# Expert results added in memory by the scatter, in two sums, in a fused mixing and MoE layer

## The reference

```
h = rmsnorm(x, norm_ffn_pre) * (1 + sc2) + sh2
y = moe_ffn(h)            # 64 experts, each token goes to 8 of them
x = x + gt2 * rmsnorm(y, norm_ffn_post)

moe_ffn: idx, gate = grouped top-8 of sigmoid(h @ w_router)
         routed[token] = sum over its 8 experts e of
                         gate * ((silu(h @ we_gate[e]) * (h @ we_up[e])) @ we_down[e])
         shared        = (silu(h @ ws_gate) * (h @ ws_up)) @ ws_down
         y = routed + shared
```

## Time and profile before

| | |
|---|---|
| runs | 1507.34, 1509.97, 1515.13 us; median 1509.97 |
| the profiled execution | 1509.81 us, of which its span is 1508.0 us |
| TensorE busy, share of the span | 1352.0 us, 90% |
| VectorE | 1045.0 us, 69% |
| ScalarE | 613.3 us, 41% |
| GpSimd | 344.7 us, 23% |
| device memory read, written | 334.40 MB, 44.04 MB |
| mean granted TensorE clock | 0.938 of full speed |

### The profile page before, as it was taken

One profiled execution on the slowest core, in us unless ns is written; L12 is line 12 of the kernel. 1 busy time (PEld: TensorE's weight loads), 2 busy tenths in 40 slices (PEclk: granted clock), 3 DMA queues, 4 the chain that ended last, 5 costly groups with the idle time before them and its releaser, 6 DMA issues. The chain is left out here.

```text
span 1508.0 us, 18807 instructions
## 1 busy us (share of the span) xinstructions
PE 1352.0 (90%) x5795; PEld 926.9 (61%) x5795; DVE 1045.0 (69%) x1646; ACT 613.3 (41%) x928; POOL 344.7 (23%) x350
## 2 busy tenths in 40 slices
PE   6799999965589799869699999999999999999947
PEld 3577676723589544344476777777777777776713
DVE  4539999959833252325688887887888888888617
ACT  3322222142123211211465565665665665655502
POOL 0344324133000000000223232232232333232200
PEclk9799999876699899979799999999999999999969
DMA  8343534110000440094289999989999988999358
GB/s 305 144 148 131 202 133 146 49 70 0 1 1 1 168 167 14 28 355 196 78 330 346 364 352 347 359 349 347 365 384 368 356 343 348 361 351 338 143 212 352
DMA packets 85841, 341.34 MB, mean 226 GB/s; under 512 B 16983, under 2 KB 20241, under 8 KB 58661
## 3 DMA queue, kind: packets, MB, share of 16 engines
q1 hardware_dynamic: 65976, 307.07, 53.2%
q0 software_dynamic: 19584, 33.60, 6.2%
q10 hardware_dynamic: 236, 0.09, 0.0%
HBM read 334.40 MB, written 44.04 MB: 251 GB/s over the span
## 5 line engine op out<-in xcount | busy, mean ns | idle before, releaser
L2144 DVE TENSOR_TENSOR gate_up_low<-gate_up,gate_up_high 128x1024 fp32r<-128x1024 f32 x204 | 245.3, 1223 | 47.2 <-ACT gate_up_high L2035 41.9
L2116 PE MATMUL py<-down_ring,hT 128*128 128x512 f32 x544 | 250.0, 602 | 0.9 <-ACT hT L2054 0.9
L2077 PE MATMUL p_gate_up<-gate_up_high,x_hi 128*128 128x512 f32 x544 | 242.7, 446 | 5.3 <-DVE x_lo L2153 5.3
L2077 PE MATMUL p_gate_up<-gate_up_low,x_hi 128*128 128x512 f32 x544 | 216.6, 398 | 0.0
L2077 PE MATMUL p_gate_up<-gate_up_high,x_lo 128*128 128x512 f32 x544 | 216.6, 398 | 0.0
L2035 ACT ACTIVATE gate_up_high<-gate_up 128x1024 fp32r<-128x1024 f32 x204 | 204.1, 1052 | 1.0 <-issue 0.8
L2116 PEld LDWEIGHTS py<-down_ring,hT 128*128 128x128 f32 x544 | 97.9, 190 | 98.8 <-issue 98.7
L2006 POOL TENSOR_TENSOR carrier<-offsets 1x1 f32<-1x1 f32 x136 | 28.7, 211 | 535.9 <-DVE tokens L2162 487.3
L269 POOL TENSOR_TENSOR ring_lo<-ring,w_hi 128x2048 fp32r<-128x2048 f32 x19 | 91.6, 4823 | 179.0 <-ACT w_hi L310 179.0
L2077 PEld LDWEIGHTS p_gate_up<-gate_up_high,x_hi 128*128 128x128 f32 x544 | 104.0, 191 | 45.6 <-issue 21.2
L429 PE MATMUL pz<-h_hi,w_hi 128*128 128x512 f32 x304 | 123.4, 406 | 7.7 <-DVE h_lo L497 7.7
(11 more groups left out here) (363 smaller groups left out, 2034.8 us busy)
## 6 DMA issues: line engine op xcount, KB each, us to landing
down_ring<-in_we_down SPq DMA_DIRECT2D x68, 1024.0 KB, 8.7
gate_up<-in_we_gate SPq DMA_DIRECT2D x51, 1024.0 KB
gate_up<-in_we_up SPq DMA_DIRECT2D x51, 1024.0 KB
ring<-in_w_ada SPq DMA_DIRECT2D x12, 2048.0 KB, 8.1
ring<-in_w_in SPq DMA_DIRECT2D x9, 2048.0 KB, 10.4
x_again<-in_we_gate SPq DMA_DIRECT2D x17, 1024.0 KB
x_again<-in_we_up SPq DMA_DIRECT2D x17, 1024.0 KB
rows<-expert_rows SPq DMA_DIRECT2D x6, 2048.0 KB, 18.4
```

The costliest lines, as they stand in the source:

```text
L2077: mm = pe.matmul(pgu[u % 2][:, :], x[:, u % 2, k, :], weights, start=(k == 0 and n == 0), stop=(k == KD - 1 and n == 2))
L2116: mm = pe.matmul(py[half][:, :], hT[:, u % 2, k, :], weights[:, k, half * N:half * N + N], start=(k == 0), stop=(k == 1))
L2144: V.tensor_tensor(moe.low[u % RING][:, :, piece(i), :], moe.gate_up[u % RING][:, :, piece(i), :], exact(w_hi[:, u % 2, :, piece(i), :]), A ...
```

## The change

- The row numbers go: the table has two values for each pair of token and expert (gate and token), and the scan, the subtraction and the four additions that built the third value are gone.
- `expert_rows` (4096 rows) is replaced by two arrays `expert_sums0` and `expert_sums1` of 512 rows. The scatter's target is the token's own row, in the first array for even blocks and the second for odd ones, and the DMA adds to what is there.
- In `route` SP first writes zeros to the second array (8 DMAs of 256 KB) ahead of the experts' first weights, and behind these weights writes the shared expert's result to the first array (4 DMAs of 512 KB, each when ScalarE has copied its tile). It waits for the zeros at the end of the stage. The first scatter waits for the shared rows.
- The residual's tile is its own and no longer a slot of the ring; in `route` it holds the shared expert's result. SP loads the residual after the weights of block 63, ahead of those of the extra blocks.
- `combine` loads two rows a token (8 DMAs of 512 KB, 4 MB in all). TensorE has no part in it. VectorE adds the two, and finishes tile t - 1 behind the sums and gates of tile t.

```diff
 # route
             sp.dma_start(wsd[:, :, :], ...)
+            sp.wait_ge(s_zero, 1)
+            for t in range(NT):
+                for half in range(2):
+                    sp.dma_start(moe.sums[1][t * P:(t + 1) * P, half * N:half * N + N], nothing).then_inc(s_clear, 16)
             for b in range(moe.RING):
                 moe.load_gate_up(sp, b, b)
                 moe.load_down(sp, b, b)
+            for t in range(NT):
+                sp.wait_ge(s_dnA, 2 * t + 2)
+                sp.dma_start(moe.sums[0][t * P:(t + 1) * P, :], shared[:, t, :]).then_inc(moe.s_base, 16)
+            sp.wait_ge(s_clear, 16 * 2 * NT)
...
+            pool.memset(nothing, 0.0).then_inc(s_zero, 1)
...
-            link(V.tensor_tensor_scan(rank[...], resets[...], sel[...], 0.0, ALU.mult, ALU.add))
-            link(V.tensor_tensor(rank[:, :, :], rank[:, :, :], sel[:, :, :], ALU.subtract))
-            for t in range(NT):
-                link.sign(V.tensor_scalar(values[:, t * NE:(t + 1) * NE, 2], rank[:, t, :], tokf[:, 2, t:t + 1], None, ALU.add))
 # experts, SP
+            sp.wait_ge(moe.s_base, 16 * NT)
+            sp.dma_start(moe.x1[:, :, :], keep.x1_dram.rearrange("(t p) d -> p t d", p=P)).then_inc(moe.s_x1, 16)
             count = sp.value_load(moe.n_blocks[0:1, 0:1], min_val=NE, max_val=MAXB)
...
-            sp.wait_ge(s_y, count)
-            sp.dma_start(moe.x1[:, :, :], keep.x1_dram.rearrange("(t p) d -> p t d", p=P)).then_inc(s_x1, 16)
-            sp.wait_ge(s_x1, 16)
 # experts, scatter
+                if isinstance(b, int) and b == 0:
+                    pool.wait_ge(moe.s_base, 16 * NT)
-                pool.indirect_dma_start(moe.rows, bass.IndirectOffsetOnAxis(row_ids[:, u % 4, 0:1], 0), y[:, u % 2, :], None,
-                                        bounds_check=last_row, oob_is_err=False).then_inc(s_out[u % 2], 16)
+                pool.indirect_dma_start(moe.sums[u % 2], bass.IndirectOffsetOnAxis(targets[:, u % 4, 0:1], 0), y[:, u % 2, :], None,
+                                        bounds_check=last_token, oob_is_err=False, compute_op=ALU.add).then_inc(s_out[u % 2], 16)
 # combine
+            for t in range(NT):
+                for i in range(2):
+                    sp.dma_start(halves[:, i, t, :], moe.sums[i][t * P:(t + 1) * P, :]).then_inc(s_in[t], 16)
...
+                V.tensor_tensor(y[:, t, cols(half)], halves[:, 0, t, cols(half)], halves[:, 1, t, cols(half)], ALU.add).then_inc(s_y, 1)
...
+            for t in range(NT):
+                dve.wait_ge(s_in[t], 32)
+                for half in range(2):
+                    add(t, half)
+                for half in range(2):
+                    gated(t, half)
+                if t:
+                    finish(t - 1)
+            finish(NT - 1)
```

More of the change, by code:

```diff
@@ L1535 @@
 MAXB = NE + S * TOPK // P - 1
-NO_TOKEN, NO_ROW = 8 * S, 16 * S * TOPK
+NO_TOKEN = 8 * S
 BIG = 1e30
@@ L1569, in route @@
         wsd, wr, g8 = old(2, D), old(KD, NE), old(NT, NG, 8)
-        scores, biased, sel, gated, left, rank, resets = (old(NT, NE) for _ in range(7))
+        scores, biased, sel, gated, left = (old(NT, NE) for _ in range(5))
         gs, top4, top8 = (m.sb(n, [P, NT, 8]) for n in ("gs", "top4", "top8"))
@@ L1573, in route @@
         gmask = m.sb("gmask", [P, NT, NG])
+        shared, nothing = moe.x1, old(N)
         total, over = m.sb("total", [P, NT]), m.sb("over", [P, NT])
-        toki, tokf, pi, pf = m.sb("toki", [P, NT], I32), m.sb("tokf", [P, 3, NT]), m.sb("pi", [P, 1], I32), m.sb("pf", [P, 1])
+        toki, tokf, pi, pf = m.sb("toki", [P, NT], I32), m.sb("tokf", [P, 2, NT]), m.sb("pi", [P, 1], I32), m.sb("pf", [P, 1])
         iota_i = m.sb("iota_i", [P, S], I32)
-        values = m.sb("table_values", [P, NT * NE, 3])
+        values = m.sb("table_values", [P, NT * NE, 2])
         colf, before = m.sb("colf4", [P, P]), m.sb("before", [P, P])
@@ L1645, in _ @@
                 for half in range(2):
-                    act.activation(moe.shared[:, t, half * N:half * N + N], bank[6 + half][:, :], ACT.Copy).then_inc(s_dnA, 1)
+                    act.activation(shared[:, t, half * N:half * N + N], bank[6 + half][:, :], ACT.Copy).then_inc(s_dnA, 1)
         @block.tensor
@@ L1849, in plan_experts @@
     moe.n_blocks = m.sb("n_blocks", [1, 1], I32)
-    moe.offsets = m.sb("offsets", [P, 2])
+    moe.offsets = m.sb("no_token", [P, 1])
     moe.s_gate_up = [m.sem(f"expert_gate_up{i}_in") for i in range(moe.RING)]
     moe.s_down = [m.sem(f"expert_down{i}_in") for i in range(moe.RING)]
-    moe.rows = nc.dram_tensor("expert_rows", (S * TOPK, D), F32, kind="Internal").ap()
+    moe.sums = [nc.dram_tensor(f"expert_sums{i}", (S, D), F32, kind="Internal").ap() for i in range(2)]
     halves = [w["we_gate"][0].rearrange("e (p k) n -> e p k n", k=KD), w["we_up"][0].rearrange("e (p k) n -> e p k n", k=KD)]
@@ L1879, in experts @@
         hot = m.sb("hot", [P, 2, NT, P], BF16)
-        column = m.sb("column", [P, 2, NT, 9], BF16)
-        number = m.sb("number", [P, 4, 3])
+        column = m.sb("column", [P, 2, NT, 6], BF16)
+        number = m.sb("number", [P, 4, 2])
         tokens = m.sb("tokens", [P, 4, 1], U32)
-        row_ids = m.sb("row_ids", [P, 4, 1], U32)
+        targets = m.sb("targets", [P, 4, 1], U32)
         x_hi, x_lo = m.sb("x_hi", [P, 2, KD, P], F32R), m.sb("x_lo", [P, 2, KD, P], F32R)
@@ L2104, in numbers @@
                 for t in range(NT):
-                    mm = pe.matmul(pid[:, 0:9], hot[:, u % 2, t, :], column[:, u % 2, t, :], start=(t == 0), stop=(t == NT - 1))
+                    mm = pe.matmul(pid[:, 0:6], hot[:, u % 2, t, :], column[:, u % 2, t, :], start=(t == 0), stop=(t == NT - 1))
                 mm.then_inc(s_id, 1)
@@ L2199, in combine @@
         whole, rstd = m.sb("whole6", [P, NT]), m.sb("rstd6", [P, NT])
[L2200 to L2205, removed]
+        s_in = [m.sem(f"p6_sums{t}_in") for t in range(NT)]
         s_y, s_gt = m.sem("p6_y"), m.sem("p6_y_gated")
@@ L2230, in _ @@
             sp.wait_ge(s_st, 16 * 2 * NT)
[L2232 to L2235, removed]
-                    pe.matmul(bank[2 * t + half][:, :], keep.ident[:, :], moe.shared[:, t, cols(half)], start=True, stop=False)
-                    pe.wait_ge(s_pe_in[t + half if t == LAST else t], 16)
-                    for j in range(H):
-                        mm = pe.matmul(bank[2 * t + half][:, :], keep.ident[:, :], rows[:, t, j, cols(half)],
-                                       start=False, stop=(j == H - 1))
-                    mm.then_inc(s_sum, 1)
         @block.gpsimd
@@ L2296, in finish @@
                                            in1=x1[:, t, cols(half)], op0=ALU.mult, op1=ALU.add).then_inc(s_o, 1)
-            for t in range(LAST):
-                dve.wait_ge(s_dve_in[t], 16)
-                tree(t, slice(0, D))
+            for t in range(NT):
+                dve.wait_ge(s_in[t], 32)
                 for half in range(2):
@@ L2304, in _ @@
                     gated(t, half)
-                finish(t)
-            for half in range(2):
-                dve.wait_ge(s_dve_in[LAST + half], 16)
-                tree(LAST, cols(half))
-                add(LAST, half)
-            for half in range(2):
-                gated(LAST, half)
-            finish(LAST)
+                if t:
+                    finish(t - 1)
+            finish(NT - 1)
 class Names:
```

67 lines of the change are left out of this document (18 added, 49 removed).

## The result

| | before | after |
|---|---|---|
| median of four runs | 1508.74 us | 1546.63 us |
| range of the runs | 1507.34 to 1515.13 | 1537.84 to 1550.87 |
| profiled execution, its span | 1509.81, 1508.0 us | 1546.62, 1544.8 us |

The ratio is 1.0229 (95% interval 1.0181 to 1.0277): slower, and the interval leaves open whether by 2%. The forecast was 1478.3 us, within 1472 to 1496, with 0.85 on faster. It was wrong by 68 us, and in sign.

What follows compares the result with a forecast made beforehand. The prediction took loads to bound the last stage and TensorE the middle stretch, with DMA at 0.92. Last stage -29.1, gap -3.0, expert stage 0 and `route` +0.4 gave -31.7 us: 1478.3 us, range 1472 to 1496.

Steps and rivals of the forecast that it cites:

- The expert stage: 0: Expert stage: no time gained or lost, since the adding scatters' extra DMA work fits under TensorE's time.
- m = 2.2: Expert stage: m is an adding scatter's cost in plain ones; above 2.2 its extra passes 0.83 us a block.
- the ring of four slots: Expert stage, DMA-bound rival: the ring holds about 10 us in reserve, taken once off the loss over 62 blocks.
- The DMA engines become the bound of the expert stage: Rival, blocks 4 to 65: slower, whole gain lost at m = 3.2, 1545 us at m = 4; chance 0.14.
- Last stage, 52.5 to 23.4 us: Last stage: fewer loads, no TensorE products, VectorE the bound after first loads; 29.1 us gained, bounds 25 to 30.
- m = 2: Expert stage: an adding scatter costs two plain ones, one more read of the same 4 KB; bounds 1 and 4.
- Mean DMA share 0.98 with TensorE at 600 of 600: Sign for "right", stretch 770 to 1370: DMA share near 0.98, TensorE still busy 600 of 600 us.
- The sign named for "wrong": Expert stage: idle before a DMA in ScalarE's weight split, or before a scatter in copies to `y`, or a DMA-entered chain.
- The gap, -3.0 us: Between last scatter and last barrier: 3.0 us less as the residual's load moves forward; bounds 0 and -3.8.
- `route`, +0.4 us: End of `route`: SP must issue the last shared write before the barrier, 0.4 us more; bounds 0 and +1.5.
- Latency of the slot, residual and clears hidden: Expert stage and `route`: slot waits, the residual's 5.9 us weight delay and the clears' about 6 us cost 0.
- The sum: Whole kernel: -29.1 - 3.0 + 0 + 0.4 = -31.7 us, giving 1478.3 us.

Runs made afterwards that it cites:

- spread_after: The changed kernel with a block's place 2m put in partition m and place 2m + 1 in partition 64 + m; 1479.59 us.
- plain_scatter: The changed kernel with plain scatters that write over the sum and add nothing, so the sums are left out; 1475.87 us.
- add_even: The changed kernel, places not dealt out, with only even blocks' scatters adding and odd blocks' writing plainly; 1508.61 us.
- two_writes: The kernel before with each scatter issued a second time, plainly, into an array nobody reads; a slot of `y` waits for both; 1592.04 us.
- two_writes_spread: The kernel before with each scatter issued twice, the second into an unread array, and place 2m in partition m, 2m + 1 in 64 + m; 1513.3 us.

## Why the prediction was wrong

**The step that failed** is the free time of DMA. The prediction says "DMA leaves 0.08 x 10.3 = 0.83 us a block free", and in "The expert stage: 0" that "DMA becomes the bound when that passes 0.83 us, at m = 2.2". The share of DMA is a mean over 16 engines, and I spent the free time of all 16 on work that falls mostly to eight. With the same rows, bytes and additions the time is 1547 us with the rows at the front and 1480 us with them spread, so the fullest engines are the bound and not the mean.

Two sizes were wrong, and both come from the mean. The added price on a busy engine is 7.5 x 0.166 = 1.25 us a block, where the mean has 0.62. And the reserve of these engines was not 0.83 us. Two doses measure it: over some 62 blocks the full dose asks for 77 us and took 67 (1547 against spread_after's 1480), the half dose asks for 39 and took 29 (1509). Both leave about 10 us in all, the once-only reserve that the prediction gives to the ring of four slots, or at most 0.16 us a block. Measured from plain_scatter's 1476 instead it is 6 us. I had put add_even in a range that supposed more.

An estimate of the fullest engine's work goes with this. The 3.15 MB of weights a block at 417 GB/s, the rate of the weight loads in 670 to 690 of the kernel before,

```profile
670.00:690.00 20.00, 19.47 (x48) 8.66 (x47) 8.93 (x71) 2.13 (x5) 0.00 (x0) 1.00 1.01 417
```

take 7.54 us on every engine. To it come, on the fullest, 7.5 gathered rows and 7.5 scattered ones of 183 or 349 ns (5.0 each when spread):

| kernel | fullest engine, worked out | a block, measured | time |
|---|---|---|---|
| before | 7.54 + 15 x 0.183 = 10.3 us | 10.3 (TensorE) | 1509 |
| after | 7.54 + 7.5 x 0.183 + 7.5 x 0.349 = 11.5 | 11.4 | 1547 |
| add_even | the mean of these two = 10.9 | 10.7 | 1509 |
| spread_after | 7.54 + 5.0 x 0.183 + 5.0 x 0.349 = 10.2 | 10.3 (TensorE) | 1480 |
| two_writes | 7.54 + 22.5 x 0.183 = 11.7 | 11.5 (52 scatters in 600 us) | 1592 |
| two_writes_spread | 7.54 + 15 x 0.183 = 10.3 | 10.3 (TensorE) | 1513 |

The estimate ranks the kernels, and its sizes are rough. In the mix the weights take more engine time than alone: in the kernel before 0.92 x 10.3 = 9.5 us of mean share less 1.4 us of rows are 8.1 us a block. With 8.1 for 7.54 each row of the table would rise by 0.6 us, above TensorE's 10.3 even where TensorE never waits. Records of a trace can be missing, too, so counts of blocks are good to one or two in a hundred.

**The rival was right in time and wrong in its reason.** "The DMA engines become the bound of the expert stage" stood at 0.14, with 1545 us at m = 4; the measured time is 1547 at m = 1.9. Its sum of 67 us takes an addition of three plain rows less 0.83 us of free time, 1.24 us a block on the mean; the fullest engines were asked for 1.25 us with no more than 0.16 to spare. That the two agree is luck. That DMA would bind, in the stage and at the cost of the whole gain, was the rival's and was right.

**Point by point.**
- *Last stage, 52.5 to 23.4 us:* right, 23.1 us; the additions take 1.28 or 1.29 us a pair (the row of 0.69 us that I read for them gave 1.38), loads 5.1 us to the first addition.
- *m = 2:* right, 1.9. The rule of the Trainium skill ("Collectives: The Full Stack", section "The bandwidth ceiling: the fold count and why AG ≠ RS ≠ AR"), that a reducing DMA runs at half a copy's rate, agrees with this price; no run here separates the read from the addition.
- *Mean DMA share 0.98 with TensorE at 600 of 600:* not in the changed kernel, but exactly what spread_after shows. The sign named in the prediction ("DMA share near 0.98") did not appear: the share fell to 0.90. The sign named for "wrong" did: idle time of the weight split before a DMA.
- *The gap, -3.0 us:* too large. In the changed kernel the gap is 1521.73 - 1509.18 = 12.6 us from the last scatter's issue, 1.2 less than before; and the issue itself comes late. The rows of the end of its expert stage:

```profile
1501.91 1.56 POOL L2021 DMA_INDIRECT expert_sums<-y,targets  x1 [0.46 <-issue]
1508.54 0.18 POOL L2003 TENSOR_TENSOR carrier<-no_token 1x1 f32<-1x1 f32 x1 [5.07 <-DMA expert_sums<-y,targets]
1509.18 1.56 POOL L2021 DMA_INDIRECT expert_sums<-y,targets  x1 [0.46 <-issue]
```
```profile
1505.21 0.69 DVE L2182 COPY y<-py 128x512 f32<-128x512 f32 x1 [4.19 <-PE py L2115]
```

  The rows were ready at 1505.9, and POOL stood until 1508.5 in the wait for the scatter before. I had looked at the gathers behind that wait and not at the next scatter. An issue takes 1.56 us instead of 0.99 too. plain_scatter, with the same order and no addition, has 1449.55 - 1439.76 = 9.8 us, which is the forecast's bound for "nothing added", 13.7 - 3.8 = 9.9. So the addition costs the last scatter 2.8 us here (3.2 in spread_after), where I had given it 0.5. POOL's row and the chain's first in plain_scatter:

```profile
1439.76 0.99 POOL L2021 DMA_INDIRECT expert_sums<-y,targets  x1 [0.46 <-issue]
```
```profile
1449.55 0.05 issue
```
- *`route`, +0.4 us:* not contradicted. From its first load to the first weight split are 718.63 - 648.51 = 70.1 us before, and 71.0, 70.5 and 70.8 us in the kernel after, spread_after and plain_scatter: 0.4 to 0.9 us more, in one profile each. The kernel after's other 2.5 us of delay arise ahead of `route`.
- *Latency of the slot, residual and clears hidden:* right where the engines are not full. spread_after has all of them and lies at 1480 us.
- *The sum:* that spread_after lies 1.3 us from the forecast is in part luck. Its gap is 0.7 us shorter than before and not 3.0, while its expert stage, from the first weight split at 722.07 to the last rows at 1436.73, takes 714.7 us against 722.3 before, where I had 0. The granted clock at the start of the stage, 719 to 770, is 0.90 in this profile and 0.83 in that of before; how much of the 7.6 us hangs on it is not shown.

The loss in sum: 11.4 - 10.3 = 1.1 us over some 62 blocks are 68 us, against the measured difference of 67 us between the changed kernel and spread_after.

## What to carry to other kernels

Before work is put on DMA engines with a few per cent to spare, ask which engines get it: a mean share of 0.92 was next to no reserve for rows that lie in half of the partitions. Where indirect transfers have fewer valid rows than partitions, try dealing them out so that every engine gets its part; here one line, which changes nothing in the computation, turned an edit that made the kernel 2.3% slower into one that makes it 1.9% faster. A finer deal, which by the map would leave 3.75 rows a block on each engine instead of 5.0 on the fullest, was not run. When the share of DMA falls while an engine begins to wait for DMA, look for unequal engines first.

## What the runs showed of the hardware that was not expected

- An indirect scatter with addition costs 349 ns of an engine's time for a row of 4 KB, against 183 ns plain (8.8% and 6.2% of the span in the software queue). Its issue on POOL takes 1.56 us against 0.99.
- Which 64 partitions hold the first 64 rows decides some 70 us: 1547 us with them in the lower half, 1551 in the upper half, 1552 in every other group of four, 1480 in the lower 32 of each half. Eight engines of sixteen, by the map cited above, fit the three slow ones.
- DMA held a mean share of 0.98 over 600 us, at 358 GB/s, without TensorE waiting once.
